# Start of a two-block transformer kernel: order of the loads, source of the conditions, place of the third modulation chunk

## What is computed

```
silu(c) @ w_mod + b_mod          -> shift, scale, gate      (tokens)
silu(c_ctx) @ w_mod + b_mod      -> shift_c, scale_c, gate_c (context)
h  = rms_norm(x, norm_g)   * (1 + scale)   + shift
hc = rms_norm(ctx, norm_g) * (1 + scale_c) + shift_c
p  = h @ w_in                     (and the same for hc)
```

## Time and profile before

| | |
|---|---|
| median of 3 runs | 2068.02 us (2066.37 to 2069.0) |
| profiled execution | 2069.35 us |
| its span, first to last instruction | 2068.0 us |
| TensorE matmul busy | 2016.2 us (97%) |
| VectorE, ScalarE, GpSimd busy | 1358.8, 827.0, 173.9 us |
| mean granted TensorE clock | 0.991 |

### The profile page before, as it was taken

How to read it: one execution, slowest core, us unless ns; L and a number is a source line. 1 busy time by engine, 2 the same in 40 slices (tenths; PEclk the granted TensorE clock), 3 DMA queues, 4 the chain that set the end, 5 groups by cost and what they waited for, 6 DMA issues and landing times.

```text
span 2068.0 us, 26264 instructions
## 1 busy us (share of the span) xinstructions
PE 2016.2 (97%) x10342; PEld 1690.6 (82%) x10342; DVE 1358.8 (66%) x1948; ACT 827.0 (40%) x1411; POOL 173.9 (8%) x177
## 2 busy tenths in 40 slices
PE   6999999999999999999999999999999999999998
PEld 2888888877888868888888888888888888888886
DVE  6678778658778766854687536657785467634454
ACT  4356555135556333134462223336224454322321
POOL 1011100111111230000000000000000000000000
PEclk9999999999999999999999999999999999999999
DMA  8322222333223356442346435434543235433332
GB/s 310 118 72 72 72 62 72 99 111 112 82 72 93 114 165 186 122 118 87 92 122 184 115 110 152 141 94 137 160 136 104 76 102 153 116 108 92 101 92 83
DMA packets 313274, 238.23 MB, mean 115 GB/s; under 512 B 6976, under 2 KB 289984, under 8 KB 312512
## 3 DMA queue, kind: packets, MB, share of 16 engines
q1 hardware_dynamic: 294000, 166.81, 27.2%
q0 software_dynamic: 18432, 67.12, 10.6%
q10 hardware_dynamic: 720, 2.62, 0.4%
HBM read 234.42 MB, written 2.10 MB: 114 GB/s over the span
## 4 chain that ended last, share of the span: by engine, by line
PE 86%; DVE 6%; ACT 3%; issue 2%; DMA 2%; SPq 0%; POOL 0%; DVEq 0%; ACTq 0%; POOLq 0%
PE ps L621 66%; PE ps L594 4%; PE ps L2607 2%; PE ps L1558 2%; PE ps L1539 1%; PE ps L1540 1%; PE ps L1569 1%; PE ps L1487 1%; PE ps L2639 1%; PE ps L2589 1%; DMA first_mod<-in_w_mod_first 1%; PE ps L2273 1%; DMA mod_w_in<-in_w_mod_turned 1%; DVE w_lo_second L577 1%; ACT a_p L1836 1%
## 5 line engine op out<-in xcount | busy, mean ns | idle before, releaser
L621 PE MATMUL ps<-h_second_hi,w_hi_second 128*128 128x512 f32 x1120 | 447.3, 399 | 1.9 <-ACT w_hi_second L557 1.9
L621 PE MATMUL ps<-h_second_lo,w_hi_second 128*128 128x512 f32 x1120 | 436.6, 390 | 0.0
L621 PE MATMUL ps<-h_second_hi,w_lo_second 128*128 128x512 f32 x1120 | 277.1, 389 | 0.4 <-DVE w_lo_second L577 0.4
L577 DVE TENSOR_TENSOR w_lo_second<-w_raw_second,w_hi_second 128x1024 fp32r<-128x1024 f32 x160 | 196.8, 1230 | 101.4 <-ACT w_hi_second L557 101.3
L621 PEld LDWEIGHTS ps<-h_second_hi,w_hi_second 128*128 128x128 f32 x1120 | 210.5, 188 | 47.8 <-ACT w_hi_second L557 2.7
L621 PEld LDWEIGHTS ps<-h_second_hi,w_lo_second 128*128 128x128 f32 x1120 | 210.1, 188 | 45.2 <-DVE w_lo_second L577 0.8
L621 PEld LDWEIGHTS ps<-h_second_lo,w_hi_second 128*128 128x128 f32 x1120 | 210.4, 188 | 44.4 <-issue 1.9
L621 PE MATMUL ps<-h_hi,w_hi_first 128*128 128x512 f32 (+1 forms) x592 | 204.9, 360 | 2.4 <-DVE proj L1925 2.3
L621 PE MATMUL ps<-h_lo,w_hi_first 128*128 128x512 f32 (+1 forms) x592 | 201.1, 353 | 0.0
L557 ACT ACTIVATE w_hi_second<-w_raw_second 128x1024 fp32r<-128x1024 f32 x168 | 176.1, 1049 | 42.3 <-PE ps L621 33.2
L621 PE MATMUL ps<-act_hi,w_hi_down 128*128 128x512 f32 x352 | 136.9, 389 | 0.0
(11 more groups left out here) (344 smaller groups left out, 3647.7 us busy)
## 6 DMA issues: line engine op xcount, KB each, us to landing
w_raw_second<-in_w_in SPq DMA_DIRECT2D x64, 512.0 KB, 4.6
w_raw_first<-in_w_in SPq DMA_DIRECT2D x48, 512.0 KB, 3.8
mod_w_mixer<-in_ada_w_turned POOLq DMA_DIRECT2D x48, 512.0 KB, 4.0
w_raw_second<-in_w_gate SPq DMA_DIRECT2D x44, 512.0 KB, 4.0
w_raw_second<-in_w_val SPq DMA_DIRECT2D x44, 512.0 KB, 4.7
w_raw_down<-in_w_down SPq DMA_DIRECT2D x32, 704.0 KB, 4.6
mod_w_ffn<-in_ada_w_turned POOLq DMA_DIRECT2D x32, 512.0 KB, 4.0
mod_w_in<-in_w_mod_turned POOLq DMA_DIRECT2D x27, 512.0 KB, 3.8
```

What stands on the lines that cost most here:

```text
L577: k.nc.vector.tensor_tensor(lo, raw, hi.bitcast(F32), ALU.subtract).then_inc(k.sem.weight_split_v, 1)
L621: last = tensor.matmul(k.ps[:, bank, 0:count], w[:, q * P:(q + 1) * P], rows[q][:, first:first + count], start=(n == 1), stop=(n == 3 * t.k))
```

## The change

SP's order becomes: columns, square constants, chunk 0 first half, start row 0, chunk 0 second half, start row 1, both halves of chunk 1, tokens in four pairs of rows, tile 0, start row 2, tile 1, start row 3, both halves of chunk 2, tables. Each half chunk and each pair has a semaphore of its own. The two broadcast loads and their two Silu passes go: TensorE turns the 16 columns of the small `act_c` tile (Silu of the conditions) into PSUM, one 128x128 transpose each, and ScalarE copies them out. VectorE makes start sums 0 and 1 before it adds squares, and start sums 2 and 3 between the low parts of rows 1 and 2 and after that of row 3. Chunk 2 is multiplied inside the first stage, after tile 0's row 0, and turned after step 1. ScalarE copies chunk 0 before the squares. In the mixers the ScalarE root and the VectorE reciprocal are replaced by a VectorE scaling and a GpSimd power of -0.5.

```diff
 def start_sync(k):
...
     sync.dma_start(k.cols[:, :], dram["columns"]).then_inc(s.columns_landed, 16)
+    sync.dma_start(k.squares[:, :, :], dram["squares"]).then_inc(s.consts_landed, 16)
+    load_first_chunk(k, 0, 0)
     load_start_rows(k, 0)
+    load_first_chunk(k, 0, 1)
     load_start_rows(k, 1)
-    sync.dma_start(k.squares[:, :, :], dram["squares"]).then_inc(s.consts_landed, 16)
-    load_first_chunk(k, 1)
+    load_first_chunk(k, 1, 0)
+    load_first_chunk(k, 1, 1)
+    for pair in range(KT // 2):
+        rows = slice(2 * pair, 2 * pair + 2)
+        sync.dma_start(k.xT[:, rows, :], dram["tokens"][:, rows, :]).then_inc(k.x_landed[pair], 16)
+    load_tile(k, 0)
     load_start_rows(k, 2)
+    load_tile(k, 1)
     load_start_rows(k, 3)
-    load_first_chunk(k, 2)
-    for u in (0, 1):
-        load_tile(k, u)
+    load_first_chunk(k, 2, 0)
+    load_first_chunk(k, 2, 1)
...
 def start_tensor(k):
...
+    for v in (0, 1):
+        for q in range(KT):
+            over = k.act_c[:, KT * v + q:KT * v + q + 1].broadcast_to([P, P])
+            last = tensor.transpose(condition_banks(k, v)[:, q * P:(q + 1) * P], over, k.ident)
+        last.then_inc(s.condition_turned, 1)
+    first_mod_tensor(k, 0, 0)
+    first_mod_tensor(k, 0, 1)
+    first_mod_tensor(k, 1, 0)
+    turn_first_mod(k, 0)
+    first_mod_tensor(k, 1, 1)
     tensor.wait_ge(s.squares_summed, 1)
...
     last.then_inc(s.norm_summed, 1)
-    first_mod_tensor(k, 1, range(4))
+    turn_first_mod(k, 1)
+    tensor.wait_ge(s.condition_ready, 2)
     tensor.wait_ge(s.norm_inverted, 1)
...
     last.then_inc(s.norm_spread, 1)
-    turn_first_mod(k, 0)
-    first_mod_tensor(k, 1, range(4, KT))
-    turn_first_mod(k, 1)
-    first_mod_tensor(k, 2, range(KT))
-    turn_first_mod(k, 2)
+
+def beside_first_rows(k, step):
+    if step == 0:
+        first_mod_tensor(k, 2, 0)
+        first_mod_tensor(k, 2, 1)
+    if step == 1:
+        turn_first_mod(k, 2)
...
 def start_scalar(k):
...
+    for v in (0, 1):
+        scalar.wait_ge(s.condition_turned, v + 1)
+        scalar.activation(k.mod_places[0][0][:, v, :], condition_banks(k, v), ACT.Copy).then_inc(s.condition_ready, 1)
+    copy_first_mod(k, 0)
     for q in range(KT):
-        scalar.wait_ge((s.x_landed0, s.x_landed1)[q // 4], 16)
+        scalar.wait_ge(k.x_landed[q // 2], 16)
...
-    silu_conditions(k, 0, 0, (0, 1))
...
 def first_rows_vector(k):
...
+    first_mod_vector(k, 0)
+    start_gain(k, 0)
     scale(0)
     scale(1)
     rest(0)
     scale(2)
-    for q in range(3, KT):
+    rest(1)
+    scale(3)
+    sum_start_rows(k, 2)
+    rest(2)
+    rest(3)
+    sum_start_rows(k, 3)
+    vector.wait_ge(s.start_summed, 2 * len(MOD_SUMS))
+    start_gain(k, 1)
+    scale(4)
+    first_mod_vector(k, 1)
+    for q in range(5, KT):
         scale(q)
-        rest(q - 2)
-    rest(KT - 2)
+        rest(q - 1)
     rest(KT - 1)
...
+def mixer_gpsimd(k, l, i):
+    s = k.sem
+    if i in (23, 27):
+        group = (23, 27).index(i)
+        k.nc.gpsimd.wait_ge(s.m_meant, 2 * l + group + 1)
+        invert_root(k, k.roots[:, 16 * group:16 * group + 16]).then_inc(s.m_inverted, 1)
...
-            vector.wait_ge(s.m_rooted, 2 * l + group + 1)
+            vector.wait_ge(s.m_squared, 8 * l + 4 * group + 4)
             roots = k.roots[:, 16 * group:16 * group + 16]
-            vector.reciprocal(roots, roots).then_inc(s.m_inverted, 1)
+            vector.tensor_scalar(roots, roots, 1.0 / P, EPS, ALU.mult, ALU.add).then_inc(s.m_meant, 1)
```

More of the change, by code:

```diff
@@ L631, in multiply_tile, with multiply_staggered @@
         multiply_part(k, u, p, ready, after)
-def multiply_staggered(k, u, lags, ready):
+def multiply_staggered(k, u, lags, ready, beside=None):
     for step in range(KT + lags[-1]):
@@ L640, in multiply_staggered @@
                     multiply_rows(k, u + n, p, (step - lag,), ready)
+        if beside:
+            beside(k, step)
 def linear_sync(k, stage, first=0):
@@ L834, in finish_early, with linear_gpsimd @@
     settle_scalar(k, scalar.activation(product, product, ACT.Identity, bias=k.early_bias[:, n:n + 1]))
-def linear_gpsimd(k, stage, then, first=0):
+def linear_gpsimd(k, stage, then, first=0, also=None):
     own = k.stage_tiles[stage]
     for i, u in enumerate(own):
+        if also:
+            also(k, stage[1], i)
         if first and i == 0:
@@ L938, in silu_conditions @@
 def silu_conditions(k, place, earlier, rows):
-    k.nc.scalar.wait_ge(k.sem.condition_landed, 16 * (earlier + len(rows)))
+    k.nc.scalar.wait_ge(k.sem.condition_landed, 16 * (earlier - 2 + len(rows)))
     for v in rows:
@@ L1377, in first_tensor @@
 def first_tensor(k, l, ready):
-    multiply_staggered(k, k.stage_tiles["in", l][0], FIRST_LAGS[l], ready)
+    multiply_staggered(k, k.stage_tiles["in", l][0], FIRST_LAGS[l], ready, None if l else beside_first_rows)
     if l:
@@ L2221, in start_sync, with load_first_chunk @@
     sync.dma_start(k.wblk[:, :, :, :, :], dram["group_weights"]).then_inc(s.group_weights_landed, 16)
[L2224 to L2227, removed]
+def load_first_chunk(k, j, half):
+    c, rows = MOD_ORDER[j], slice(half * KT // 2, (half + 1) * KT // 2)
+    source = k.dram["w_mod_first"].rearrange("(k p) n -> p k n", p=P)[:, rows, c * MOD_COLS:(c + 1) * MOD_COLS]
+    k.nc.sync.dma_start(k.mod_chunks[j][:, rows, :], source).then_inc(k.first_mod_landed[j][half], 16)
 def load_start_rows(k, m):
@@ L2251, in start_tensor, with condition_banks, first_mod_tensor @@
     last.then_inc(s.norm_spread, 1)
[L2252 to L2256 removed]
+def beside_first_rows(k, step):
[4 more added lines that the diff above has]
+        turn_first_mod(k, 2)
+def condition_banks(k, v):
+    return k.banks(4 * v, D)
 def first_mod_product(k, j):
[L2260 removed]
+    return k.ps[0:2, (2, 3, 3)[j], :]
 def first_mod_columns(k, j):
[L2264 to L2267 removed]
+    return k.ps[:, (7, 7, 6)[j], 8 * (j % 2):8 * (j % 2) + 2 * MOD_BLOCKS]
+def first_mod_tensor(k, j, half):
     s, tensor = k.sem, k.nc.tensor
[L2270 to L2272 removed]
+    tensor.wait_ge(k.first_mod_landed[j][half], 16)
+    for q in range(half * KT // 2, (half + 1) * KT // 2):
         last = tensor.matmul(first_mod_product(k, j), k.act_c[:, q:2 * KT:KT], k.mod_chunks[j][:, q, :],
                              start=(q == 0), stop=(q == KT - 1))
[L2275 removed]
+    if half:
         last.then_inc(s.first_mod_product, 1)
@@ L2297, in first_mod_vector, with start_gain @@
                                         k.column("b_mod", first, 4), ALU.add)
-    settle_vector(k, last)
+    last.then_inc(s.first_shift_ready, 1)
+    vector.wait_ge(s.first_shift_ready, half + 1)
+def start_gain(k, half):
     first_norm_gain(k, 0, 4 * half, 4)
-    vector.wait_ge(s.norm_gain_ready, 2 * half + 2)
+    k.nc.vector.wait_ge(k.sem.norm_gain_ready, 2 * half + 2)
 def start_scalar(k):
```

57 lines of the change are left out of this document (16 added, 41 removed).

## The result

The changed kernel took 2074.48 us, the median of 7 runs (2072.08 to 2075.35), beside 2068.16 us (2065.72 to 2070.15, 7 runs) of the kernel before on the same chip: a ratio of 1.0031 with a 95% interval of 1.0022 to 1.0040. It is 6.3 us slower. The forecast was 2070.7 with a range of 2064.9 to 2072.9, so both the size and the range were missed. The profiled execution took 2075.35, the longest of the seven; its span is 2074.0.

What follows compares the result with a forecast made beforehand. TensorE, holding 86% of the chain, was taken as the bound. 39.6 (row 0) + 17.6 + 8.0 + 2.65 - 65.1 = +2.7 us, mixers 0, on 2068.0 gave 2070.7 us, range 2064.9 to 2072.9.

Steps and rivals of the forecast that it cites:

- Landings: Load queue at the start: each load lands at 3.3 us + KB/392, first tokens at 19.7, chunk 2 at 36.0.
- TensorE until the tokens: Start: condition transposes, chunk 0 to near 16, chunk 1 with turn to near 24; all free, covered by waiting for tokens.
- The norm: First norm: VectorE's eight adds of squares take 8.40 us after tokens land, so TensorE's norm sums start at 29.2.
- The clock decides: TensorE idles five us before the norm sums; its clock falls to half, and the spread is ready at 35.6.
- Light records: TensorE's 26 short norm records (sums, chunk 1's turn, spreads): 6.4 us at half speed, against 3.4 at full clock.
- Rival A: TensorE keeps or regains full clock at the start: tiles 0 and 1 end at 62.2, time 2065.1; chance 0.20.
- C: Chunk 2 beside row 0 pays back the early start, with a shorter low spell: +0.5, 2068.5; chance 0.13.
- Rows: After the spread: row 0 at 39.6, then 17.6 row work, 8.0 chunk 2 and turn, 2.65 half clock; end 67.8.
- cover of 1.9 us: Row 4 of the first stage: ready at 56.0, TensorE reaches it at 57.9, so no wait there.
- Rival B: GpSimd's second split holds up VectorE within row 0 for 2.2 us: +4.9, 2072.9; chance 0.15.
- Mixers: Replacing ScalarE roots and reciprocals by VectorE scaling and GpSimd power changes 0; loss at most 8.8 us.
- What follows is dense TensorE work in an unchanged order: After tiles 0 and 1: any shift of their end shifts the kernel's end equally, forecast +2.7 us.

Runs made afterwards that it cites:

- 2: The changed kernel without the mixer edit (the new start alone): 2072.7 us, ratio 1.0025 to the kernel before.
- experiment 3: The changed kernel with both idle TensorE stretches filled by repeated products of chunk 0, 12 and 8 records, results unused: 2069.47 us, ratio 1.0008.
- 4: The changed kernel with only the first idle stretch, ahead of the norm sums, filled by repeated products: 2071.54 us, ratio 1.0023.
- 5: The changed kernel with only the second idle stretch, between spread and row 0, filled by four repeated products: 2070.39 us, ratio 1.0012.
- kernel 10: The changed kernel with the table of constants loaded behind chunk 0's first half instead of ahead of it: 2070.25 us, ratio 1.0010.
- kernel 7: The changed kernel with token pair 0 in front, chunks and tokens loaded in turn, start sums drawn forward, chunk 2 ahead of row 0: 2065.19 us, ratio 0.9990.
- kernel 11: Kernel 7 with the table of constants loaded behind token pair 0: 2061.87 us, ratio 0.9972.
- 1: The kernel before with the mixer edit alone (VectorE scaling and GpSimd power): 2066.75 us, ratio 1.0004.
- kernel 9: The changed kernel with four token pairs loaded ahead of chunk 0; start sums 0 and 1 and chunk 0's copy behind the squares: 2073.37 us, ratio 1.0028.
- kernel 8: Kernel 7 with repeated products ahead of both halves of chunk 1: 2065.34 us, ratio 0.9995.
- 6: The changed kernel with chunk 2 multiplied ahead of row 0, chunks and tokens loaded in turn, start sums after the squares: 2067.0 us, ratio 0.9997.

## Why the prediction was wrong

Its yardstick, the end of tiles 0 and 1, was to be 67.8 and came at 69.53. By its own steps:

- **Landings: the step that failed first.** "Landing is then 3.3 us + KB/392" gave token pair 0 at 19.7; it came at 22.12, 2.4 late. The rate was nearly right: the fifteenth of sixteen completions came at 20.1. What the sum left out is that a load is there when its slowest engine is through, and that this engine can lag. It read the 392 KB/us off a queue that begins with tokens, and kept it for one that begins with the table; the 16.9 and 29.5 that agreed with the old rows tested the rate and not the new order. The size of the miss is in part that of one execution: in kernels 2 to 5, with the same order of loads, the tokens released ScalarE at 20.3 to 21.7, so 0.6 to 2.0 late. That a later table makes the kernel faster is shown by the times of two pairs (the changed kernel and 10, 7 and 11). That it does so by the lag is not shown: kernel 10 speaks for it (0.5 us), kernel 11 doesn't (1.9 us, within the nine of before). What makes a part lag stays open.
- **TensorE until the tokens: nearly right.** Chunk 1 with its turn was to end near 24; it ended at 26.2, since chunk 0's half came at 9.64 and not 7.3. The cover took it.
- **The norm: right.** From the tokens to the norm sums 9.5 us were forecast, 9.52 measured.
- **The clock decides: right in kind and near in size.** Experiments 3, 4 and 5 show it by filling the stretches. Light records 6.4 forecast, 6.0 measured. The Trainium skill (TensorE: Matmul & The Clock Gate, "HAM oscillation — how this bites in real kernels") warns of just such bursts parted by waits, and here the trace agrees: 0.50 from 36 to 44. Rival A (the clock holds) is refuted, and C, with its shorter low spell, too.
- **Rows: right.** Spread to row 0: 4.0 forecast, 4.1 measured. From row 0 to the fold 28.25 (17.6 + 8.0 + 2.65) forecast, 27.8 measured; the loss to half clock was 2.4 in experiment 3's comparison, against 2.65. There was no hole before row 4, as the cover of 1.9 us had it. GpSimd's second split (41.26 to 43.8) met the low part at 42.5 and made it 2.2 us, as the prediction allowed, beside chunk 2. Rival B, a split inside row 0, did not come.
- **Mixers: right as far as it can be seen,** by experiments 1 and 2: no wait in the first edited mixer, and no cost that shows in a ratio known to 0.2%.
- **Sum.** 67.8 + 2.4 (tokens) + 0.1 (spread to row 0) - 0.4 (light records) - 0.4 (row 0 to the fold) = 69.5, the measured 69.53. The stage closes.
- **"What follows is dense TensorE work in an unchanged order, so a shift there is a shift of the end": the second step that failed.** The stage lost 4.4 us, the medians differ by 6.3. From the fold to the end the profiled executions took 2003.0 before and 2004.7 after, so 1.7 lie there. The low-clock windows of later norms and mixers fall differently, as over 300 to 460 us, first of the kernel before, then of the one after:

```profile
300.00:460.00 160.00, 152.09 (x902) 133.00 (x901) 116.28 (x173) 55.83 (x101) 20.20 (x16) 0.99 0.27 81
```

```profile
300.00:460.00 160.00, 153.00 (x895) 134.34 (x894) 119.12 (x176) 57.23 (x106) 17.34 (x14) 0.96 0.24 73
```

  The clock's mean is 0.99 and 0.96. But in the eleven other kernels this remainder is between 1999.9 and 2005.2, and it doesn't follow the fold: 2003.1 in kernel 10, 1999.9 in kernel 9, which has the changed kernel's rows. The five kernels with the changed order of loads untouched (the changed one, 2, 3, 4 and 5) have 2003.2 to 2005.2, the others 1999.9 to 2003.1. The kernel before alone scattered from 2063.9 to 2070.6 us in the 34 runs beside 4, 5, 7 and 8. Whether the remainder holds a real cost of some 1 or 2 us or the chance of one execution each is open; no run was made for it.

The range failed with both steps. The stage ended 1.7 us behind the forecast 67.8; added to 2070.7 that is 2072.4, still inside. Of the 2.1 us from there to 2074.5, 1.7 lie behind the fold, and 0.4 are the different distances of the two profiled executions from their medians. The range was widened for the clock and for GpSimd, whose mechanisms were seen, and not for the landings, which were held for known, nor for what follows the fold; one more term of 0 to 2.5 us would have carried the upper end from 2072.9 past the measured 2074.5. The cheaper hint stood in the rows: the loads in front of the queue had changed in size and kind, and no row of before showed such a queue's first 10 us.

## What to carry to other kernels

A load is as late as its slowest part: when the first loads of a kernel are reordered, bound the landing by the spread of completions and not only by bytes over rate, and try a small table behind the first large load where the critical path waits for what follows; here that helped twice, by a way that is not settled. Moving weights ahead of activations spreads TensorE's work out; count the idle stretches that this makes, since each may cost what follows at half clock, and fill them with real work (chunk 2 ahead of row 0) rather than put that work behind the wait. Once TensorE's wait is gone, look who is next: here VectorE's order of sums and rows set the end.

## What the runs showed of the hardware

The lag between the 16 parts of one load was the surprise: 0.8 us in the kernel before, 3.0 in the changed kernel, 3.3 in kernel 7, 0.5 in kernel 10, 1.9 in kernel 11. In the changed kernel it stayed the same, 2.9 to 3.1, for every load of the next 25 us (22.1 against 19.1 at token pair 0). The Trainium skill (DMA: Bandwidth & Descriptors, "Why a DMA increments its semaphore by 16 and not by 1") says that the engines "finish independently, and the semaphore counts them"; the completions here agree.

Work on GpSimd stopped VectorE. VectorE's timeline in kernel 7, two records of 128x4 that took 0.23 us in kernel 10:

```profile
35.15 1.55 DVE L2431 SCALAR_TENSOR_TENSOR norm_gain<-mod,cols 128x4 f32<-128x4 f32 x2
```

and GpSimd's in the same kernel:

```profile
34.27 2.33 POOL L569 TENSOR_TENSOR w_lo_first<-w_raw_first,w_hi_first 128x1024 fp32r<-128x1024 f32 x1 [33.82 <-ACT w_hi_first L559]
```

The records end when the split ends, at 36.6 to 36.7. The same 1.3 us were lost in experiments 3, 6, 8 and 9, 0.5 in 11 and 0.2 in 4, where the norm was ready before the split was done: a gain upstream moved VectorE into GpSimd's work. The Trainium skill (SBUF — State Buffer, "Terms") has VectorE and GpSimd share a pair of ports that is held for a whole instruction; for these records the trace agrees. Not every VectorE record beside a split is held up: in the changed kernel the scaling of a row, with one input in PSUM, took its usual 1.13 us at 41.49, during the second split, and the low part behind it, with its inputs in SBUF, 2.22 us instead of 1.14.

The clock can fall in the middle of the light records. In experiments 4 and 11 it was full at the norm sums (1.50) and half at the spread (1.54 for what takes 0.87), with an idle time of 0.67 us and of none before the sums; in kernel 7 it held through the same records. Nor does the length of a wait settle it: a wait of 1.8 us for `h_lo` was followed by the fall to 0.50 in kernel 7 and by none in kernel 8. What decides between the two was not tested.
